# Two transformer blocks on one core: attention A moved off GpSimd, with its steps cut and ordered anew

## The chip, the core and the metric

The kernel runs on one core of a Trainium2 chip. The engines are named as the profile names them: PE (TensorE, matrix products into the eight banks of PSUM, ps0 to ps7), DVE (VectorE), ACT (ScalarE), POOL (GpSimd), and SP (SyncE), which issues all DMAs here. Each engine works through its own list of instructions in order and stops at a wait on a semaphore; nothing behind the waiting instruction can pass it. The metric is the time of one execution in microseconds (us), lower is better.

## What is computed

The first block has a layer with differential attention ("attention A"), a feed-forward part, a layer with banded attention ("attention B"), and another feed-forward part. The second block has a gated mixer and a feed-forward part. The sequence has 512 rows of 1024 features. The change touches attention A:

```python
def diff_attention(x, w_qkv, lam_params, subln_g, w_o, lambda_init):
    qkv = x @ w_qkv                       # 8 heads, each with two q/k halves of 64 and v of 128
    q = apply_rope(q, cos, sin) * (A_HEAD_DIM ** -0.5)      # * 0.125
    k = apply_rope(k, cos, sin)
    for i in range(s // Q_BLOCK):         # 4 blocks of 128 queries, keys 0 .. 128*(i+1)
        sc = jnp.einsum('bqhmd,bkhmd->bhmqk', q[:, q0:kend], k[:, :kend])
        p = jax.nn.softmax(jnp.where(allowed, sc, neg), axis=-1)
        a = p[:, :, 0] - lam * p[:, :, 1]
        outs.append(jnp.einsum('bhqk,bkhe->bqhe', a, v[:, :kend]))
    o = rms_norm(o, subln_g) * (1.0 - lambda_init)
    return o.reshape(b, s, D_MODEL) @ w_o
```

Its output is added to the scaled input, and a layer norm follows.

## The kernel before

Every weight matrix is read in tiles of 128 x 1024 numbers (512 KB). A tile is split in two on the chip: ACT rounds it to `whi` (the step `split`, L989), DVE forms the remainder `wlo` (L1269), and PE multiplies three times (L527 to L529): high by high, and the two mixed products. Activations are split in the same way (`xh`, `xl`, `hh`, `hl`). Six places hold split tiles, and splits are issued four tiles ahead of their use.

A class `Plan` writes one list of steps for all engines. Each engine walks the whole list and emits its own share of each step, so the order of the list is the order of every engine's program. In attention A the list is woven from two strands.

The filler strand is made of pieces. Each piece is six matmuls of 512 columns. The q projection of a head takes four pieces, the k projection four more; after the heads' projections come groups of the output product with `a_w_o` ("rows", one block of 256 inputs for one block of 128 rows per piece). When a projection is done, the step `post` applies the rotation: DVE multiplies the PSUM bank by the sine table in two halves into `tmp` (L1297, L1298) and by the cosine table into q or k (L1301); POOL adds the two (L1616). For q, POOL then makes two copies that are masked by halves (L1621, L1624), since the two softmaxes of a head share one product of full height. Each `post` is followed by a `split` of a later tile.

The attention strand is the table `ORDER_A`, run once for each head; a dash stands for one piece of filler, a small letter for a step of the head before:

- `S0` to `S3`: the scores of query block i. PE makes two products of 128(i+1) columns (L783), DVE blanks a corner (L1451), takes row maxima (L1454) and scales them by -0.125 (L1457), ACT takes the exponentials with their sums (L1132).
- `F0` to `F3`: the shares. DVE inverts the sums (L1465), multiplies one by minus lambda (L1468), scales the first exponential (L1469) and adds the second, scaled (L1472).
- `T0` to `T3` (`t3` for the head before): PE transposes the shares (L793), ACT copies them out of PSUM (L1139).
- `w`: PE multiplies v by the transposed shares (L803), ACT squares the result (L1149).
- `n`: PE sums the squares with a matrix of ones (L813), ACT forms the inverse root (L1155, L1157), DVE scales the head by it (L1478), ACT rounds the head to `hh` (L1159), DVE forms `hl` (L1480).

A bank is taken in rotation; those that gather over several steps (projections, output rows, the result of `w`) are held and skipped. Before PE writes a bank it waits for the operation that read it last; for the bank of `w` that is L1478 (the semaphore `of`). `AHEAD_A` pieces of filler run before the first head's turn. After the last head come the output product's remaining rows and the layer norm.

Of the kernel before, what the change touches and what calls it, by code (L numbers as in the profile page):

```python
# [10 lines left out]
ALU = mybir.AluOpType  # L11
ACT = mybir.ActivationFunctionType
AX = mybir.AxisListType.X
# [15 lines left out]
AHEAD_A = 8  # L29
ORDER_A = "- t3 - S0 S1 F0 w F1 - T0 S2 T1 S3 F2 - - - F3 n T2 -".split()  # L30
# [20 lines left out]
class Plan:  # L51
# [152 lines left out]
    def rows(self, kind, source, row0, nk, k_first=0, hh=True, norm=None, group=0):  # L204
# [3 lines left out]
        for nh in range(2):  # L208
            ends = nh == 1 and norm is not None
            if ends:  # L210
                runs = [blocks]
                self.step("table", SQRT)
            elif nh == 1:
                runs = [[k] for k in blocks[:-n]] + [blocks[-n:]]
            else:
                runs = [[k] for k in blocks]
            out, taken = {}, {}
            for run in runs:
                for t in range(4):
                    if ends and t == 3:  # L220
                        self.waiting = True
                    for k0 in run:
                        first, last = k0 == blocks[0], k0 == blocks[-1]
                        if first and (t == 0 or ends):
                            for u in [t] if ends else range(4):
                                out[u] = Rows(kind, nh, u, self.bank(hold=True), self.count(kind), norm, group)
                        if ends and norm >= 4 and last and t == 3:
                            self.feat(norm, 1)
                            self.xsplit(norm, 1)
                            self.step("ln", norm, 2)  # L230
                        if t == 0:
                            taken[k0] = self.take("rows", *source, row0 + k0, nh)
                        r = out[t]
                        signal = last or t == 3
                        ready = max(self.h[k0], self.h[k0 + 1]) if hh else None
                        self.step("rows", r, k0, taken[k0], first, last, signal, ready)
                        if signal:
                            r.value = self.count("rows") + 1
                        if t == 3:
                            self.done(taken[k0], "rows", r.value)  # L240
                        if ends and first and t == 3 and norm >= 4:
                            self.feat(norm, 0)
                            self.xsplit(norm, 0)
                        elif ends and first and t >= 2 and norm < 4:
                            self.feat(norm, t - 2)
                            self.xsplit(norm, t - 2)
                            if t == 3:
                                self.step("ln", norm, 2)
                        if last:
                            self.held.discard(r.bank)  # L250
                            self.step("rows_post", r)
                            if ends and t < 2:
                                if norm >= 4 and t == 1:
                                    self.step("yscale", norm, 0)
                                self.step("ln", norm, t)
                            elif ends and t == 2 and norm >= 4:
                                self.step("yscale", norm, 1)
                        yield
# [1586 lines left out]
```

## Time and profile before

| What | Value |
|---|---|
| time before, median of 3 runs | 1864.07 us (1862.79 to 1864.3) |
| the profiled execution's own time | 1865.22 us |
| its span, first to last instruction | 1863.5 us |
| mean granted clock of PE | 0.995 |
| PE busy | 1819.0 us, 98% |
| DVE busy | 903.0 us, 48% |
| ACT busy | 654.3 us, 35% |
| POOL busy | 65.9 us, 4% |
| DMA | 176.6 MB, mean 95 GB/s |

The span leaves 1.7 us of the profiled time outside it. PE is busy nearly throughout; the places where it is not are short and lie for the most part in the first 260 us. Busy time says which engine has work, not who waits for whom; for that the waits and the chain are read, stretch by stretch.

### The profile page before, as it was taken

The page shows a single profiled execution, that of the slowest core. Times are in us where ns is not written, and L with a number is a line of the kernel's source. Part 1 is how long each engine was busy: PE and PEld are TensorE (multiplying, and loading weights), DVE is VectorE, ACT ScalarE, POOL GpSimd, SP SyncE. Part 2 cuts the span into 40 slices and gives each one's busy share as a digit, 9 for nine tenths or more (in the row PEclk, how much of TensorE's full clock was granted, in tenths as well). Part 3 has the DMA queues.
Part 4 walks back from the last instruction along what each step waited for, and adds up shares of the span by engine and source line. Part 5 has one row for each costly group of instructions (what it writes and reads, how often), then busy time and mean ns, then how long its engine had stood idle before and what let it go on. Part 6 is the DMA issues. An engine that isn't in the chain of part 4 may idle for free.

```text
span 1863.5 us, 21342 instructions
## 1 busy us (share of the span) xinstructions
PE 1819.0 (98%) x8624; PEld 1464.8 (79%) x8624; DVE 903.0 (48%) x1540; ACT 654.3 (35%) x1080; POOL 65.9 (4%) x68
## 2 busy tenths in 40 slices
PE   8989889999999999999999999999999999999998
PEld 6766669888888896666788888888877798888886
DVE  3588865333333634555743333338343573334343
ACT  4344433312222234554232231233445453323241
POOL 0332200000000000000000000000000000000000
PEclk9999999999999999999999999999999999999999
DMA  8322232333423342222233323353221424242321
GB/s 273 108 74 79 72 90 69 102 91 102 113 79 94 121 125 74 80 68 62 69 102 102 91 93 100 101 148 92 63 68 57 124 92 112 70 113 79 102 90 46
DMA packets 217881, 176.60 MB, mean 95 GB/s; under 512 B 8963, under 2 KB 177829, under 8 KB 217782
## 3 DMA queue, kind: packets, MB, share of 16 engines
q1 hardware_dynamic: 217782, 175.23, 31.3%
q8 instruction: 69, 1.13, 0.3%
q14 instruction: 30, 0.25, 0.0%
HBM read 173.07 MB, written 7.38 MB: 97 GB/s over the span
## 4 chain that ended last, share of the span: by engine, by line
PE 91%; DVE 6%; ACT 2%; issue 1%; DMA 0%; SPq 0%
PE ps L527 27%; PE ps L529 27%; PE ps L528 27%; PE ps L823 2%; PE ps L833 1%; PE ps L783 1%; PE ps L845 1%; DVE wlo L1269 1%; PE ps L722 1%; DVE stat L1454 1%; PE ps L934 0%; DVE arena L1301 0%; DVE arena L1297 0%; DVE arena L1298 0%; PE ps L793 0%
## 5 line engine op out<-in xcount | busy, mean ns | idle before, releaser
L527 PE MATMUL ps<-xh,whi 128*128 128x512 f32 (+1 forms) x1176 | 442.3, 376 | 0.0
L529 PE MATMUL ps<-xh,wlo 128*128 128x512 f32 (+1 forms) x1176 | 431.4, 367 | 0.0
L528 PE MATMUL ps<-xl,whi 128*128 128x512 f32 (+1 forms) x1176 | 431.0, 367 | 0.0
L1269 DVE TENSOR_TENSOR wlo<-raw,whi 128x1024 fp32r<-128x1024 f32 x236 | 285.5, 1228 | 272.6 <-ACT whi L989 272.1
L989 ACT ACTIVATE whi<-raw 128x1024 fp32r<-128x1024 f32 x236 | 244.5, 1051 | 133.3 <-PE ps L529 104.4
L527 PE MATMUL ps<-whi,hh 128*128 128x512 f32 x648 | 256.4, 396 | 5.5 <-DVE hl L1480 3.7
L529 PE MATMUL ps<-whi,hl 128*128 128x512 f32 x648 | 253.0, 390 | 0.0
L527 PEld LDWEIGHTS ps<-xh,whi 128*128 128x128 f32 x1176 | 222.7, 189 | 38.4 <-issue 4.5
L528 PE MATMUL ps<-wlo,hh 128*128 128x512 f32 x648 | 252.9, 390 | 0.0
L529 PEld LDWEIGHTS ps<-xh,wlo 128*128 128x128 f32 x1176 | 221.9, 189 | 36.9
L528 PEld LDWEIGHTS ps<-xl,whi 128*128 128x128 f32 x1176 | 222.2, 189 | 36.4 <-issue 2.9
L527 PEld LDWEIGHTS ps<-whi,hh 128*128 128x128 f32 x648 | 122.4, 189 | 32.1 <-issue 7.7
L529 PEld LDWEIGHTS ps<-whi,hl 128*128 128x128 f32 x648 | 122.0, 188 | 25.8
L528 PEld LDWEIGHTS ps<-wlo,hh 128*128 128x128 f32 x648 | 122.2, 189 | 24.9 <-issue 0.5
L527 PE MATMUL ps<-xh,extra 128*128 128x512 f32 (+1 forms) x328 | 116.2, 354 | 2.0 <-DVE xl L1282 2.0
L529 PE MATMUL ps<-xh,extra 128*128 128x512 f32 (+1 forms) x328 | 115.7, 353 | 0.0
L528 PE MATMUL ps<-xl,extra 128*128 128x512 f32 (+1 forms) x328 | 115.7, 353 | 0.0
L1346 DVE SCALAR_TENSOR_TENSOR x<-x,ps 128x512 f32<-128x512 f32 x64 | 43.9, 685 | 114.9 <-PE ps L529 114.9
L1011 ACT ACTIVATE arena<-ps 128x512 f32<-128x512 f32 x44 | 26.3, 598 | 199.4 <-PE ps L529 199.4
L1014 ACT ACTIVATE hh<-arena 128x512 fp32r<-128x512 f32 x44 | 27.8, 632 | 194.9 <-DVE arena L1307 194.9
L1269 DVE TENSOR_TENSOR extra<-raw,extra 128x1024 fp32r<-128x1024 f32 x53 | 64.5, 1222 | 56.4 <-ACT extra L989 56.4
L527 PE MATMUL ps<-whi,xh 128*128 128x512 f32 x192 | 78.7, 410 | 8.4 <-DVE wlo L1269 8.4
(200 smaller groups left out, 2117.2 us busy)
## 6 DMA issues: line engine op xcount, KB each, us to landing
raw<-in_ffn_w_in SPq DMA_DIRECT2D x88, 512.0 KB, 4.0
raw<-in_w_ff SPq DMA_DIRECT2D x64, 512.0 KB, 4.2
raw<-in_ffn_w_out SPq DMA_DIRECT2D x44, 512.0 KB, 3.8
raw<-in_a_w_qkv SPq DMA_DIRECT2D x24, 512.0 KB, 5.1
raw<-in_w_in SPq DMA_DIRECT2D x20, 512.0 KB, 3.8
raw<-in_kv_w SPq DMA_DIRECT2D x16, 512.0 KB, 4.6
bias_skewed<-bias_rows SPq DMA_DIRECT2D x8, 640.0 KB
raw<-in_a_w_o SPq DMA_DIRECT2D x8, 512.0 KB, 5.2
```

Source lines behind the costliest of these rows:

```text
L527: e.matmul(o, ah, bh, start=start, stop=False)
L528: e.matmul(o, ah, bl, start=False, stop=False)
L529: return e.matmul(o, al, bh, start=False, stop=stop)
L722: m = e.transpose(ps[b][:, k * 128:k * 128 + 128], src[:, c:c + 128], ident[:])
L783: e.matmul(ps[b][:, 0:n], q[:, i * 128:i * 128 + 128], k[:, 0:n], start=True, stop=True).then_inc(s.scores, 1)
L823: e.matmul(ps[b][:, 0:n], q[c, i * 128:i * 128 + 128], k[c, 0:n], start=True, stop=True).then_inc(s.scores_b, 1)
L833: m = e.transpose(ps[b][:, j * 128:j * 128 + 128], e_[:, j * 128:j * 128 + 128], ident[:])
L989: e.activation(self.parts(m)[0], self.raw[:, m % RAW, :], ACT.Copy).then_inc(s.hi, 1)
L1011: e.activation(self.silu_out[n % 2], ps[b][:], ACT.Silu).then_inc(s.silu, 1)
L1014: e.activation(self.hh[:, job.arg[-1], :], self.h_out[n % 2], ACT.Copy).then_inc(s.hh, 1)
L1269: e.tensor_tensor(lo, self.raw[:, m % RAW, :], f32(hi), ALU.subtract).then_inc(s.lo, 1)
L1346: e.scalar_tensor_tensor(x[:, t, c], x[:, t, c], 1.0 if r.group else ALPHA, ps[b][:], ALU.mult, ALU.add).then_inc(s.res, 1)
```

## The change

All of GpSimd's share of attention A moves. DVE adds the two parts of the rotation itself (L1330 of the changed kernel), behind the three multiplications. ACT makes the two masked copies of q (L1018, L1020), and the masks now hold 0.125, so that the scores come out scaled. The row maxima are written negated by the reduction itself, one for each of the two scores, and the multiplication by -0.125 falls away. The shares are cut in two steps: `R` (DVE inverts and multiplies by minus lambda, then ACT scales the first exponential, L1154) and `F` (DVE adds the second). The end of a head is cut in three: `n` (PE's sum and ACT's inverse root), `m` (DVE's scaling, ACT's rounding, and the bank of `w` given back to the rotation) and `l` (`hl`). The table has eight dashes instead of seven, and four pieces run ahead instead of eight.

The output product's order is written as one list; in attention A three pieces of its second half are drawn before the last four of its first half, so that 15 pieces of it, not 12, can fill attention A. The order within the other stages stays, but for the loading of ACT's square-root table (later by three pieces) and the numbers of the banks.

```diff
-AHEAD_A = 8
-ORDER_A = "- t3 - S0 S1 F0 w F1 - T0 S2 T1 S3 F2 - - - F3 n T2 -".split()
+AHEAD_A = 4
+ORDER_A = "- t3 - S0 S1 w R0 R1 - F0 F1 T0 S2 n - T1 - R2 m S3 F2 - - T2 l R3 F3 -".split()
...
         blocks = [(k_first + k) % nk for k in range(0, nk, 2)]
         n = min(3, len(blocks))
-        for nh in range(2):
...
+        left = [(0, t, k) for k in blocks for t in range(4)]
+        if norm is not None:
+            right = [(1, t, k) for t in range(4) for k in blocks]
...
+        order = left[:-4] + right[:3] + left[-4:] + right[3:] if early else left + right
...
-        out = self.rows("res", ("a_w_o", 0), 0, 8, norm=1)
+        out = self.rows("res", ("a_w_o", 0), 0, 8, norm=1, early=True)
...
-            for _ in range(12):
+            for _ in range(15):
...
                 elif name == "n":
-                    self.step("norm_a", g, av[g], self.bank(), self.block(g))
+                    self.step("norm_a", g, self.bank())
+                elif name == "m":
+                    self.step("heads_a", g, av[g], self.block(g))
                     self.held.discard(av[g])
+                elif name == "l":
+                    self.step("low_a", g, self.h[g] - 1)
...
+                elif name[0] == "R":
+                    self.step("ratios_a", g, int(name[1]))
...
-                if job.kind == "gate":
+                if job.kind == "q_a":
+                    h = job.arg
+                    q0, q1, _ = self.qk_a[h % 3]
+                    w.wait_ge(s.rope, 2 * h + 1)
+                    w.wait_ge(s.mask, 16)
+                    e.activation(q1, q0, ACT.Copy, scale=self.masks[:, 1:2]).then_inc(s.half, 1)
+                    w.wait_ge(s.half, h + 1)
+                    e.activation(q0, q0, ACT.Copy, scale=self.masks[:, 0:1]).then_inc(s.halves, 1)
+                elif job.kind == "gate":
...
                 for m, b in enumerate(banks):
-                    w.wait_ge(s.nb, z + 1)
+                    w.wait_ge(s.nb, 2 * z + m + 1)
...
-                                 bias=self.stat[:, c + 2 + m:c + 3 + m], scale=0.125,
+                                 bias=self.stat[:, c + 2 + m:c + 3 + m],
...
+            elif what == "ratios_a":
+                h, i = arg
+                z, e0 = 4 * h + i, self.e_a[(4 * h + i) % 2][0][:, 0:(i + 1) * 128]
+                w.wait_ge(s.ratio, z + 1)
+                e.activation(e0, e0, ACT.Copy, scale=self.stat[:, 8 * z + 6:8 * z + 7]).then_inc(s.share0, 1)
...
                     e.tensor_tensor(dst, ps[b][:], self.cosb, ALU.mult).then_inc(s.cos, 1)
+                    w.wait_ge(s.dve, own)
+                    w.wait_ge(s.cos, u + 1)
+                    e.tensor_tensor(dst, dst, self.tmp, ALU.add).then_inc(s.rope, 1)
...
-                    e.reduce_max(stat[:, c + m:c + m + 1], ps[b][:, 0:n], AX).then_inc(s.dve, 1)
-                    own += 1
-                w.wait_ge(s.dve, own)
-                e.tensor_scalar(stat[:, c + 2:c + 4], stat[:, c:c + 2], -0.125, None, ALU.mult).then_inc(s.nb, 1)
+                    e.tensor_reduce(stat[:, c + 2 + m:c + 3 + m], ps[b][:, 0:n], AX, ALU.max,
+                                    negate=True).then_inc(s.nb, 1)
+
+            elif what == "ratios_a":
+                h, i = arg
+                z = 4 * h + i
+                r = stat[:, z * 8 + 6:z * 8 + 8]
+                w.wait_ge(s.exp, 2 * z + 2)
+                e.reciprocal(r, stat[:, z * 8 + 4:z * 8 + 6]).then_inc(s.ratio, 1)
+                w.wait_ge(s.ratio, z + 1)
+                e.tensor_tensor(r[:, 1:2], r[:, 1:2], self.nlam, ALU.mult).then_inc(s.ratio1, 1)
...
-                e.tensor_scalar(e0, e0, r[:, 0:1], None, ALU.mult).then_inc(s.dve, 1)
-                own += 2
-                w.wait_ge(s.dve, own)
-                e.scalar_tensor_tensor(e0, e1, r[:, 1:2], e0, ALU.mult, ALU.add).then_inc(s.p, 1)
...
+                w.wait_ge(s.share0, z + 1)
+                w.wait_ge(s.ratio1, z + 1)
+                e.scalar_tensor_tensor(e0, e1, stat[:, z * 8 + 7:z * 8 + 8], e0, ALU.mult, ALU.add).then_inc(s.p, 1)
+
+            elif what == "heads_a":
+                h, b, block = arg
                 w.wait_ge(s.rstd, h + 1)
                 w.wait_ge(s.hl, h)
                 e.scalar_tensor_tensor(self.of_a, ps[b][:], self.g8, self.sq_a, ALU.mult, ALU.mult).then_inc(s.of, 1)
+
+            elif what == "low_a":
+                h, block = arg
...
-            elif what == "post" and arg[0].kind in ("q_a", "k_a"):
...
-                e.tensor_tensor(dst, dst, self.tmp, ALU.add).then_inc(s.rope, 1)
...
-                    e.tensor_scalar(q1, q0, self.masks[:, 1:2], None, ALU.mult).then_inc(s.pool, 1)
...
-                    e.tensor_scalar(q0, q0, self.masks[:, 0:1], None, ALU.mult).then_inc(s.halves, 1)
```

The first place is ACT's program between two heads in the middle of attention A. Before, from the split behind `S3` to the exponentials of the next `S0` and `S1` (L1132 exponential, L989 `whi` of a tile, L1155 to L1159 the end of a head, L1139 copy of transposed shares):

```order
L989 ACTIVATE whi<-raw 128x1024 [waits s_job,s_raw0]
L1155 ACTIVATE arena<-ps5,small 128x512 [waits s_ss]
L1157 ACTIVATE arena<-arena 128x512 [waits s_ss_ln]
L1159 ACTIVATE hh<-arena 128x512 [waits s_of]
L1139 ACTIVATE arena<-ps6 128x3x128 [waits s_turn]
L1139 ACTIVATE arena<-ps7 128x4x128 [waits s_turn]
L989 ACTIVATE whi<-raw 128x1024 [waits s_job,s_raw1]
L1132 ACTIVATE arena,stat<-ps1,stat 128x128 [waits s_nb]
L1132 ACTIVATE arena,stat<-ps2,stat 128x128
L1132 ACTIVATE arena,stat<-ps3,stat 128x256 [waits s_nb]
L1132 ACTIVATE arena,stat<-ps4,stat 128x256
```

Of the change (L1159 and L1146 are now the copy and the exponential, L1154 the scaling of a share, L1018 and L1020 the masked copies, L995 `whi`):

```order
L1159 ACTIVATE arena<-ps1 128x3x128 [waits s_turn]
L1154 ACTIVATE arena<-arena,stat 128x512 [waits s_ratio]
L1018 ACTIVATE arena<-arena,small 128x512 [waits s_rope]
L1020 ACTIVATE arena<-arena,small 128x512 [waits s_half]
L995 ACTIVATE whi<-raw 128x1024 [waits s_job,s_raw1]
L1159 ACTIVATE arena<-ps3 128x4x128 [waits s_turn]
L1146 ACTIVATE arena,stat<-ps4,stat 128x128 [waits s_nb]
L1146 ACTIVATE arena,stat<-ps5,stat 128x128 [waits s_nb]
L1146 ACTIVATE arena,stat<-ps6,stat 128x256 [waits s_nb]
L1146 ACTIVATE arena,stat<-ps7,stat 128x256 [waits s_nb]
L1169 ACTIVATE arena<-ps0 128x512 [waits s_av]
L1154 ACTIVATE arena<-arena,stat 128x128 [waits s_ratio]
```

The two masked copies, which wait for the rotation of q, now stand ahead of `whi`, and `whi` ahead of the copy for the last transpose, on which `w` waits. The scaling for `F3` stands behind the copy for `T2`.

The second place is PE's program in one head, from `w` to the scores of `S3`. Before (L803 `w`, L793 transposes, L783 scores, L527 the first matmul of a piece's group):

```order
L803 MATMUL ps6<-arena 128x512 [waits s_cos,s_at]
...
L793 MATMUL ps0<-ident,arena 128x128 [waits s_p]
L783 MATMUL ps1<-arena 128x384
L783 MATMUL ps2<-arena 128x384 [waits s_exp]
L793 MATMUL ps3<-ident,arena 128x128 [waits s_exp,s_p]
...
L783 MATMUL ps4<-arena 128x512 [waits s_exp]
L783 MATMUL ps5<-arena 128x512 [waits s_exp]
L527 MATMUL ps7<-xh,whi 128x512
```

Of the change (L809 `w`, L799 transposes, L789 scores, L819 the sum of squares, L532 the filler):

```order
L809 MATMUL ps2<-arena 128x512 [waits s_exp,s_at]
...
L799 MATMUL ps3<-ident,arena 128x128 [waits s_p]
L789 MATMUL ps5<-arena 128x384
L789 MATMUL ps6<-arena 128x384 [waits s_exp]
L819 MATMUL ps7<-arena,ones 128x512 [waits s_exp,s_square]
L532 MATMUL ps4<-xh,whi 128x512
...
L799 MATMUL ps0<-ident,arena 128x128 [waits s_exp,s_p]
...
L532 MATMUL ps1<-xh,whi 128x512 [waits s_exp,s_lo]
...
L789 MATMUL ps2<-arena 128x512 [waits s_of]
L789 MATMUL ps3<-arena 128x512 [waits s_at]
L532 MATMUL ps1<-xh,whi 128x512
```

Before, no score of this head writes the bank of `w`, ps6. Of the change, `S3` takes ps2, the bank that `w` wrote for the head before, and waits for `of`; four pieces stand between `w` and it, and PE has nothing else it may do while it waits.

## Rows read from the trace of the kernel before

**Rows 1.** The page, part 1: busy us (share of the span) and instructions.

```profile
PE 1819.0 (98%) x8624; PEld 1464.8 (79%) x8624; DVE 903.0 (48%) x1540; ACT 654.3 (35%) x1080; POOL 65.9 (4%) x68
```

**Rows 2.** By stretch: length, busy time (instructions), clock, DMA share, GB/s.

```profile
54.70:257.00 202.30, 179.93 (x746) 128.71 (x744) 157.86 (x374) 88.09 (x215) 54.10 (x32) 0.98 0.25 78
257.00:1863.50 1606.50, 1592.71 (x7688) 1298.04 (x7688) 727.08 (x1146) 545.74 (x843) 10.79 (x28) 1.00 0.31 91
```

**Rows 3.** Waits of PE in attention A: us in total, times, longest.

```profile
PE ps L793 <- DVE arena L1472: 5.9, 7, 1.3
PE ps L813 <- DVE arena L1301: 5.1, 3, 2.3
PE ps L527 <- DVE hl L1480: 3.7, 1, 3.7
```

**Rows 4.** Timeline of DVE, two posts: start, us, [idle <-releaser].

```profile
71.18 0.69 DVE L1297 TENSOR_TENSOR arena<-ps,arena 64x512 f32<-64x512 f32 x1 [2.21 <-PE ps L529]
...
76.62 0.69 DVE L1297 TENSOR_TENSOR arena<-ps,arena 64x512 f32<-64x512 f32 x1 [2.21 <-PE ps L529]
```

**Rows 5.** The chain of waits in order of time: start us, us, what.

```profile
190.39 1.72 PE ps L783 x4
...
198.25 1.07 DVE stat L1468
...
247.45 2.21 PE ps L803 x8
...
253.32 0.70 ACT arena L1155
254.04 0.64 ACT arena L1157
254.70 0.76 DVE arena L1478
255.48 0.64 ACT hh L1159
256.15 0.70 DVE hl L1480
```

**Rows 6.** DVE groups while POOL rests: count | busy, mean ns | idle.

```profile
L1269 DVE TENSOR_TENSOR wlo<-raw,whi 128x1024 fp32r<-128x1024 f32 x3 | 3.7, 1226 | 2.5 <-ACT whi L989 2.5
...
L1472 DVE SCALAR_TENSOR_TENSOR arena<-arena,stat 128x512 f32<-128x512 f32 x2 | 1.5, 751 | 0.1
L1454 DVE TENSOR_REDUCE stat<-ps 128x1 f32<-128x512 f32 x2 | 1.4, 691 | 0.1
...
L1468 DVE TENSOR_TENSOR stat<-stat,small 128x1 f32<-128x1 f32 x4 | 0.6, 159 | 0.1
...
L1454 DVE TENSOR_REDUCE stat<-ps 128x1 f32<-128x128 f32 x2 | 0.6, 292 | 0.1
```

**Rows 7.** Groups of ACT in the same stretch.

```profile
L989 ACT ACTIVATE whi<-raw 128x1024 fp32r<-128x1024 f32 x4 | 4.2, 1049 | 0.0
...
L1149 ACT ACTIVATE arena<-ps 128x512 f32<-128x512 f32 x2 | 1.2, 598 | 3.1 <-PE ps L803 3.1
...
L1139 ACT ACTIVATE arena<-ps 128x384 f32<-128x384 f32 x2 | 0.9, 474 | 0.0
L1132 ACT ACTIVATE arena<-ps,stat 128x256 f32<-128x256 f32 x2 | 0.9, 470 | 0.5 <-DVE stat L1457 0.5
```

**Rows 8.** DVE groups from 70 to 275 us, all shapes together.

```profile
L1469 DVE TENSOR_SCALAR arena<-arena,stat 128x128 f32<-128x128 f32 (+3 forms) x32 | 15.6, 488 | 0.0
...
L1468 DVE TENSOR_TENSOR stat<-stat,small 128x1 f32<-128x1 f32 x32 | 8.7, 272 | 1.2
L1457 DVE TENSOR_SCALAR stat<-stat 128x2 f32<-128x2 f32 x32 | 7.2, 226 | 1.1
```

**Rows 9.** Busy time by stretch, just after two long waits of PE.

```profile
219.00:222.50 3.50, 3.41 (x8) 2.17 (x9) 2.36 (x4) 1.30 (x2) 1.26 (x1) 0.54 0.02 5
...
256.40:260.00 3.60, 3.02 (x8) 2.42 (x9) 1.74 (x3) 3.57 (x4) 0.00 (x0) 0.53 0.09 22
```

More of the change, by code:

```diff
@@ L200, in projections, with rows @@
             self.run(self.quarters(*w))
-    def rows(self, kind, source, row0, nk, k_first=0, hh=True, norm=None, group=0):
+    def rows(self, kind, source, row0, nk, k_first=0, hh=True, norm=None, group=0, early=False):
         blocks = [(k_first + k) % nk for k in range(0, nk, 2)]
         n = min(3, len(blocks))
-        for nh in range(2):
+        left = [(0, t, k) for k in blocks for t in range(4)]
+        if norm is not None:
+            right = [(1, t, k) for t in range(4) for k in blocks]
+        else:
+            right = [(1, t, k) for k in blocks[:-n] for t in range(4)] + [
+                (1, t, k) for t in range(4) for k in blocks[-n:]]
+        order = left[:-4] + right[:3] + left[-4:] + right[3:] if early else left + right
+        out, taken = {}, {}
+        for nh, t, k0 in order:
+            first, last = k0 == blocks[0], k0 == blocks[-1]
@@ L209, in rows @@
             ends = nh == 1 and norm is not None
-            if ends:
-                runs = [blocks]
+            if first:
+                out[nh, t] = Rows(kind, nh, t, self.bank(hold=True), self.count(kind), norm, group)
+            if ends and last and t == 0:
                 self.step("table", SQRT)
[L213 to L258, printed above, removed]
@@ new lines, in rows @@
+            if ends and first and t == 3:
+                self.waiting = True
+            if ends and norm >= 4 and last and t == 3:
+                self.feat(norm, 1)
+                self.xsplit(norm, 1)
+                self.step("ln", norm, 2)
+            if t == 0:
+                taken[nh, k0] = self.take("rows", *source, row0 + k0, nh)
+            r, tile = out[nh, t], taken[nh, k0]
+            signal = last or t == 3
+            ready = max(self.h[k0], self.h[k0 + 1]) if hh else None
@@ new lines, in rows @@
+            self.step("rows", r, k0, tile, first, last, signal, ready)
+            if signal:
+                r.value = self.count("rows") + 1
+            if t == 3:
+                self.done(tile, "rows", r.value)
+            if ends and first and t == 3 and norm >= 4:
+                self.feat(norm, 0)
+                self.xsplit(norm, 0)
+            elif ends and first and t >= 2 and norm < 4:
+                self.feat(norm, t - 2)
+                self.xsplit(norm, t - 2)
+                if t == 3:
+                    self.step("ln", norm, 2)
@@ L260, in half_rows @@
+            if last:
+                self.held.discard(r.bank)
+                self.step("rows_post", r)
+                if ends and t < 2:
+                    if norm >= 4 and t == 1:
+                        self.step("yscale", norm, 0)
+                    self.step("ln", norm, t)
+                elif ends and t == 2 and norm >= 4:
+                    self.step("yscale", norm, 1)
+            yield
     def half_rows(self, kind, col):
@@ L1151, in scalar @@
             elif what == "norm_a":
-                h, _, b, block = arg
+                h, b = arg
                 w.wait_ge(s.eps, 2)
@@ L1296, in vector @@
                         w.wait_ge(s.rope, u)
[L1297 to L1298 removed]
+                    e.tensor_tensor(self.tmp[0:64, :], ps[b][64:128, :], self.sinb[64:128, :],
+                                    ALU.mult).then_inc(s.dve, 1)
+                    e.tensor_tensor(self.tmp[64:128, :], ps[b][0:64, :], self.sinb[0:64, :],
+                                    ALU.mult).then_inc(s.dve, 1)
+                    own += 2
                     if h >= 3:
@@ L1607, in gpsimd @@
                 before = (s.ext, 1)
-            elif what == "post" and arg[0].kind in ("q_a", "k_a"):
-                job = arg[0]
-                h, which = job.arg, int(job.kind == "k_a")
-                q0, q1, k = self.qk_a[h % 3]
-                dst, u = k if which else q0, 2 * h + which
-                w.wait_ge(*before)
-                w.wait_ge(s.cos, u + 1)
-                e.tensor_tensor(dst, dst, self.tmp, ALU.add).then_inc(s.rope, 1)
-                before = (s.rope, u + 1)
-                if not which:
-                    w.wait_ge(s.mask, 16)
-                    w.wait_ge(s.rope, u + 1)
-                    e.tensor_scalar(q1, q0, self.masks[:, 1:2], None, ALU.mult).then_inc(s.pool, 1)
-                    own += 1
-                    w.wait_ge(s.pool, own)
-                    e.tensor_scalar(q0, q0, self.masks[:, 0:1], None, ALU.mult).then_inc(s.halves, 1)
-                    before = (s.halves, h + 1)
             elif what == "bias":
```

21 lines of the change are left out of this document (7 added, 14 removed).

## The prediction

> **What bounds the kernel now.** I read busy time first: PE 1819 of 1863.5 us, 98% [rows 1]. The change cannot shorten PE's work, since every product stays, so all that can move is PE's waiting. The busy time by stretch says where that is: from 257 us on PE is idle 13.8 us in 1606; in attention A, 54.7 to 257 us, it is idle 22.4 in 202.3, while DVE works 157.9 us there, 78% [rows 2]. The waits name DVE: 5.9 us for the share (L1472) before the transposes, 5.1 us in 3 waits where PE needs the bank that the rotation (L1301) had yet to read, and 3.7 us once at the end, for `hl` of the last head [rows 3]. So attention A is a loop in which PE and a crowded DVE wait for one another, and everything behind it only shifts.
>
> **What the change takes from DVE.** Out go the scaling of the first exponential, 15.6 us in 32, and of the maxima, 7.2 us [rows 8]. In come 16 sums of 512 columns; L1480, with two inputs in SBUF of that size, took 0.70 [rows 5], so 11.2. Net 11.6 us. POOL costs DVE something too: L1468 took 1.07 us once, beside 0.16 while POOL rests, and 0.27 in the mean [rows 5, 6, 8]; its 32 alone hold 3.6 us of that, and I put all such stretching of the remaining instructions at 4 to 7 us. DVE's work falls from 158 to about 140 us. POOL's path (about 50 us of work) is gone.
>
> The Trainium skill ("SBUF — State Buffer", Who interferes with whom) has DVE and GpSimd share a port pair as an exclusive lock; the row of 1.07 agrees. "Perfetto Trace Analysis" (Optimizing Scalar/DVE Operations) advises moving work from a saturated DVE to ScalarE. By that rule alone PE's waits for DVE would shrink, the first rival below.
>
> **What it adds, and where it waits.** ACT gets 16 masked copies and 32 scalings, about 25 us on 88 [rows 2]. ACT has room in the sum, but not in order. I follow one full head (1 to 6), from its `T0` to the next one's. A result reaches the next engine 0.03 to 0.06 us after its record's end; behind a matmul I add 0.2. A piece is 1.36 us: two posts start 5.44 us apart with four pieces between [rows 4].
>
> 1. PE: `T0` 0.1, `S2` 1.3 (three quarters of the 1.72 of `S3`), `n` 0.86, the fourth piece of k 1.36, 0.2 to land: 3.8 [rows 4, 5].
> 2. DVE: rotation of k, four times 0.69, 2.75; `wlo` 1.22; two small ones 0.36; `m` 0.76: 5.1 [rows 4 to 6]. In DVE's order `m` stands behind the post and the split.
> 3. PE: `S3` takes the bank of `w` and waits for `m`. PE reached it four pieces after `w`, at 16.4 us of the head, and `m` ends at 20.2: PE idles 3.8 us. Then `S3` 1.7, about 0.4 until matmuls run at pace behind it, two pieces 2.7, `T2` and landing 0.5: 5.4.
> 4. ACT copies `T2` 0.47 and only then scales for `F3`, 0.64 (as L1157); DVE adds, 0.75; gaps 0.1: 2.0 [rows 5 to 7].
> 5. DVE rotates q: 2.75.
> 6. ACT makes the two masked copies, which wait for the finished rotation: 1.3 with a gap. Only then comes `whi` 1.05; DVE, standing at `wlo`, waits 2.4 us, then 1.22: 3.7 [rows 6, 7]. Behind `whi` stands also the copy of `t3`, so `w` on PE starts 2.1 us late. Before, POOL masked beside all this and `whi` waited for nothing.
> 7. DVE blanks and reduces `S0` and `S1`: 2 x 0.29, 2 x 0.43 (between 0.29 and 0.69), 4 x 0.16: 2.1 [rows 6].
> 8. ACT: last exponential with its sum 0.7 [0.47 in rows 7], the square 0.6, the scaling 0.3; DVE's add 0.35; gaps: 2.0. `T0` comes 1.2 us late.
>
> Sum 26.8 us a head. PE's own work in it: 8 pieces 10.9, scores 4.3 (1.72 x 10/4), `w` 2.2, transposes 1.1, `n` 0.86: 19.3 [rows 4, 5]. So 7.5 us of waiting a head.
>
> The scaling on ACT shows nowhere before for SBUF operands; the bounds are 0.28 to 0.48 (the PSUM copy of up to 384 columns, 0.47, [rows 7]) and 0.64 for 512 columns, and I take 0.3 for 128 columns and 0.64 for 512. The masked copies lie between 0.60 (L1149) and 0.64 (L1157); I take 0.64. Either end moves a head by 0.2 us.
>
> **The sum.** Twelve pieces ahead of head 0 (8 of its own, 4 of `AHEAD_A`): 16.3. Head 0, with no `t3`, `w`, `n`: PE work 15.8, and 6.1 of waiting, since its first maxima stand behind rotation, masks, `whi` and `wlo` of q of head 1: 21.9. Six heads: 161. Head 7 and the end: 11 pieces 15.0, attention 8.4, `T3`, `w` and `n` of the head before 3.5, `S3` waiting for `m` 3.4, the end's chain ACT 0.70, 0.64, DVE 0.76, ACT 0.64, DVE 0.70 and 0.8 around it, 4.2 [rows 5]: 34.6. The end's chain is hidden no better than before: all 15 pieces are used up before `n`. Together 233.8 us, up to the first row block that needs the last head, where before took 202.3 [rows 2]. Three pieces more are done by then, 4.1 us. Net +27.4. The layer norm's first rows follow its sums closer than before (one piece instead of four between): 0 to +1.5, taken as 0.
>
> PE's clock: after two of PE's long waits (2.3 and 3.7 us) the stretches of 3.5 us show it at 0.54 and 0.53, close to 1.2 GHz instead of 2.4 [rows 9], and each costs up to 1.7 us of work. The stage before holds two such falls; mine has eight waits of 3 us or more. Bounds 0 and 13.6; I take two again, 3.4, because some long waits of before left the clock alone. The Trainium skill ("TensorE: Matmul & The Clock Gate", HAM oscillation — how this bites in real kernels) warns of repeated idle gaps; by it the sum would take the upper bound, 1905.
>
> The profiled execution took 1865.22, 1.15 over the median. 1865.22 + 27.4 + 3.4 - 1.15 = 1894.9, so 1895.
>
> **The rivals.**
> A. Faster, by the port and the lighter DVE. DVE's 140 us fit well under PE's work, and PE's waits for DVE (the 5.9 and 5.1 of [rows 3] and some 5 more) go, with a fall of the clock: 1864 - 16 - 2 = 1846. It needs the masked copies and `m` to end before they are asked for. Against it: DVE would be idle when PE asks, and steps 3 and 6 are waits of order, not of load. Chance 0.13.
> B. Slower, but only by one of the two order waits. If `S3` finds its bank free (a post ending earlier), 2.6 us a head go (the wait, less what steps 3 and 4 would then meet at DVE) over seven heads: 1895 - 18 = 1877. Chance 0.25.
> C. The two cancel: 3 us a head lost, as many won by the port. 1864, chance 0.05.
> D. The clock falls in nearly every head, 13.6 instead of 3.4: 1905. Counted with the forecast, together 0.57.
>
> The change does what it says in any of these; that it wouldn't has no chance of its own.
>
> The range: 1867 to 1908 leaves out most of A and C below and a little above. A measurement of this kernel tells 0.2%, 3.7 us, from no change. Faster by more 0.13, within 0.05, slower 0.82.
>
> **What would show it.** PE waiting for DVE's `m` (L1507) before L789 of 512 columns, over 3 us, in heads 1 to 7: step 3. ACT idle before L1018, DVE idle 2.4 us before L1292 with ACT's L995 as releaser, once a head: step 6. PE waiting for ACT's L1159 at L809. Rows L1330 at 0.69. The squares' products (L819) 26 to 28 us apart. L1493 at 0.16 throughout: the port. DVE busy near 140 us in the stage. If L789 never waits for L1507, step 3 is wrong; if `wlo` follows the rotation at once, step 6 is; if heads stand 20 us apart, A holds.

## The result

| | before | after |
|---|---|---|
| time, median | 1863.94 us | 1907.02 us (1906.5 to 1908.51, 4 runs) |
| ratio to before | | 1.0234, 95% interval 1.0216 to 1.0251 |
| profiled execution, its span | 1865.22, 1863.5 us | 1908.51, 1906.8 us |
| mean granted clock of PE | 0.995 | 0.983 |
| attention A, from 54.7 us to the first product that needs the last head | 202.3 us | 249.6 us |
| PE idle in it | 22.4 us | 47.3 us |
| half-clock stretches in it | 3, 10.2 us | 12, 51.2 us |

The half-clock stretch at the end of the stage is counted whole, though most of it lies behind the end. The change is slower by 43.1 us, 12 us more than the 1895 forecast and inside the range. Part 1 of the page after, as [rows 1]:

```profile
PE 1837.3 (96%) x8624; PEld 1473.4 (77%) x8624; DVE 887.6 (47%) x1492; ACT 684.8 (36%) x1128; POOL 11.8 (1%) x36
```

PE's busy time rose by 18.3 us with the same 8624 products; POOL's fell from 65.9 to 11.8. Where, the stretches tell, as in [rows 2]:

```profile
54.70:304.30 249.60, 202.25 (x764) 140.43 (x762) 144.77 (x328) 120.68 (x266) 0.00 (x0) 0.90 0.22 68
304.30:1906.80 1602.50, 1588.76 (x7670) 1294.87 (x7670) 724.72 (x1144) 543.66 (x841) 10.77 (x28) 1.00 0.31 91
```

Behind attention A the program takes 1602.5 us, before 1606.5: it has three pieces less to do (4.1 us at 1.36). So all of the loss lies in the stage: 249.6 - 202.3 - 4.1 = 43.2. Of this, idle time of PE is 47.3 - 22.4 = 24.9, and longer busy time 202.2 - 179.9 - 4.1 = 18.2. The second part goes with the clock, 0.90 in the mean, before 0.98. The waits of PE, from 50 to 310 us, as [rows 3]:

```profile
PE ps L789 <- DVE arena L1507: 22.5, 7, 3.5
PE ps L809 <- ACT arena L1159: 11.9, 6, 2.0
PE ps L799 <- DVE arena L1501: 6.9, 4, 4.6
PE ps L532 <- DVE hl L1512: 3.7, 1, 3.7
PE ps L799 <- DVE arena L1327: 2.3, 1, 2.3
```

`S3` waits for `m` in seven heads (3.5 us in six, 1.6 in the last), `w` for the copy of `t3` in six. What DVE itself waits for:

```profile
DVE wlo L1292 <- ACT whi L995: 26.8, 14, 3.2
DVE ps L1480 <- PE ps L789: 26.3, 24, 2.2
DVE arena L1501 <- ACT arena L1154: 24.2, 15, 3.0
```

The first of these in the kernel before, from 50 to 310 us too:

```profile
DVE wlo L1269 <- ACT whi L989: 9.5, 12, 3.3
```

DVE, which was crowded before, now stands and waits: for `whi` 26.8 us instead of 9.5, for PE's scores 26.3, for ACT's scaling 24.2. Two stretches of the stage, the wait of one `S3` and what follows it (columns as in [rows 2]; compare [rows 9]):

```profile
143.00:146.80 3.80, 0.34 (x2) 0.00 (x0) 3.60 (x7) 1.13 (x2) 0.00 (x0) 1.00 0.00 0
146.80:150.30 3.50, 3.48 (x5) 1.51 (x5) 0.80 (x2) 1.07 (x2) 0.00 (x0) 0.51 0.59 147
```

PE did 0.34 us of work in 3.8, at full clock, and then ran 3.5 us at half clock (1.2 of 2.4 GHz). The chain of waits through most of this head:

```profile
144.70 1.13 DVE wlo L1292
...
146.02 0.76 DVE arena L1507
...
146.82 3.65 PE ps L789 x4
...
153.61 0.49 ACT arena L1159
154.10 0.62 ACT arena L1154
...
155.53 0.69 DVE arena L1320
...
157.77 0.70 DVE arena L1330
...
158.50 0.73 ACT arena L1018
...
159.27 0.60 issue
159.88 1.05 ACT whi L995
...
160.95 1.23 DVE wlo L1292
```

The head's time is a single file of steps from engine to engine: `wlo`, `m` (L1507), `S3` (L789), the copy of `T2` (L1159) and the scaling behind it (L1154), the rotation of q (L1320 to L1330), the masked copies (L1018; L1020 lies in the 0.60 shown as issue), `whi`, `wlo`. And the rows that answer to the bounds, with count, busy time and mean ns:

```profile
L1330 DVE TENSOR_TENSOR arena<-arena 128x512 f32<-128x512 f32 x12 | 8.3, 692 | 1.3
...
L1493 DVE TENSOR_TENSOR stat<-stat,small 128x1 f32<-128x1 f32 x29 | 4.6, 159 | 1.0
```

```profile
L1154 ACT ACTIVATE arena<-arena,stat 128x512 f32<-128x512 f32 x8 | 5.7, 714 | 0.0
...
L1018 ACT ACTIVATE arena<-arena,small 128x512 f32<-128x512 f32 x6 | 4.3, 722 | 22.7 <-DVE arena L1330 22.7
L1020 ACT ACTIVATE arena<-arena,small 128x512 f32<-128x512 f32 x6 | 4.3, 721 | 0.2
...
L1154 ACT ACTIVATE arena<-arena,stat 128x128 f32<-128x128 f32 x7 | 2.8, 396 | 0.0
```

### The profile page after: what moved, and what is told of

Its sections match the earlier page's. It is cut to its first block, busy times and chain, and to the rows that moved or that the text cites. A ratio compares the mean times of both kernels' runs of the same rounds, so it can differ in the third digit from the quotient of the medians.

```text
span 1906.8 us, 21339 instructions
## 1 busy us (share of the span) xinstructions
PE 1837.3 (96%) x8624; PEld 1473.4 (77%) x8624; DVE 887.6 (47%) x1492; ACT 684.8 (36%) x1128; POOL 11.8 (1%) x36
## 4 chain that ended last, share of the span: by engine, by line
PE 91%; DVE 5%; ACT 2%; issue 1%; DMA 0%; SPq 0%; DVEq 0%
PE ps L532 27%; PE ps L534 27%; PE ps L533 27%; PE ps L829 2%; PE ps L789 2%; PE ps L839 1%; PE ps L851 1%; PE ps L728 1%; PE ps L809 1%; DVE wlo L1292 1%; ACT whi L995 1%; DVE arena L1327 1%; DVE arena L1320 1%; DVE arena L1322 1%; DVE arena L1330 0%
## 5 line engine op out<-in xcount | busy, mean ns | idle before, releaser
L532 PE MATMUL ps<-xh,whi 128*128 128x512 f32 (+1 forms) x1176 | 449.1, 382 | 0.0
L995 ACT ACTIVATE whi<-raw 128x1024 fp32r<-128x1024 f32 x236 | 244.3, 1050 | 121.8 <-PE ps L534 89.7
L532 PE MATMUL ps<-whi,hh 128*128 128x512 f32 x648 | 257.3, 397 | 5.5 <-DVE hl L1512 3.7
L532 PEld LDWEIGHTS ps<-xh,whi 128*128 128x128 f32 x1176 | 224.5, 191 | 41.3 <-issue 7.4
L532 PEld LDWEIGHTS ps<-whi,hh 128*128 128x128 f32 x648 | 122.4, 189 | 32.8 <-issue 8.5
L532 PE MATMUL ps<-xh,extra 128*128 128x512 f32 (+1 forms) x328 | 116.2, 354 | 2.0 <-DVE xl L1305 2.0
L532 PE MATMUL ps<-whi,xh 128*128 128x512 f32 x192 | 78.9, 411 | 8.5 <-DVE wlo L1292 8.5
```

The lines of the kernel that those rows point to most:

```text
L532: e.matmul(o, ah, bh, start=start, stop=False)
L995: e.activation(self.parts(m)[0], self.raw[:, m % RAW, :], ACT.Copy).then_inc(s.hi, 1)
```

## The experiments

The theory: two waits of order make the loss, `S3` for the bank of `w` and `whi` behind the masked copies, and the clock adds to them. A rival: the work moved to ACT and DVE costs time wherever it stands. Another: the new order itself costs time. Line numbers differ from kernel to kernel; the letters of the steps are the same. "Late masks" is this step: ACT's masked copies leave `post` and stand as their own step `M` ahead of `R2`. For each run the table shows the stage as above, from 54.7 us to the first product that needs the last head. "Slower pace" is busy time over 176.2 us, which the tenth experiment's profile needed with no half-clock stretch, less 4.1 where three more pieces lie in the stage. The figure is good to about 1 us: experiment 11 comes out at -0.8. Each profile is of one execution, which can lie up to 4 us from the median in its row (that of 10 took 1858.0 us, that of 8 1865.5). A half-clock stretch that begins within 1.5 us of the end of the stage is counted whole.

| kernel | median us | ratio, 95% interval | PE idle | slower pace | half-clock stretches us |
|---|---|---|---|---|---|
| before | 1863.94 | | 22.4 | 3.7 | 10.2 |
| the change | 1907.02 | 1.0216 to 1.0251 | 47.3 | 21.9 | 51.2 |
| 1 bank | 1882.37 | 1.0081 to 1.0112 | 32.9 | 8.5 | 20.5 |
| 2 late masks | 1884.68 | 1.0095 to 1.0126 | 35.6 | 10.8 | 27.3 |
| 3 both | 1863.81 | 0.9989 to 1.0008 | 20.5 | 4.3 | 13.7 |
| 4 old order | 1884.34 | 1.0093 to 1.0123 | 34.2 | 10.1 | 23.9 |
| 5 is 3, scaling on DVE | 1861.23 | 0.9973 to 0.9991 | 20.5 | 2.1 | 17.1 |
| 6 is 3, early scores of head 0 | 1856.70 | 0.9948 to 0.9973 | 17.7 | 0.8 | 6.8 |
| 7 is 4, scaling on DVE | 1875.91 | 1.0049 to 1.0076 | 28.0 | 5.1 | 17.1 |
| 8 before, negated maxima | 1863.03 | 0.9979 to 0.9997 | 18.1 | 5.2 | 17.1 |
| 9 is 1, masks on POOL | 1860.45 | 0.9967 to 0.9986 | 17.9 | 0.9 | 6.8 |
| 10 is 7, late masks | 1861.73 | 0.9982 to 1.0000 | 20.4 | 0 | 0 |
| 11 is 3, 5 and 6 | 1858.02 | 0.9954 to 0.9979 | 18.0 | -0.8 | 6.8 |
| 12 is 11, two pieces behind `w` | 1875.75 | 1.0046 to 1.0072 | 32.6 | 2.7 | 10.2 |

**1. The bank of `w` kept from `S3`.** The bank goes back to the rotation only once `S3` has taken its two:

```diff
-                    self.held.discard(av[g])
+                    if h == 8:
+                        self.held.discard(av[g])
...
                     self.step("scores_a", g, int(name[1]), [self.bank(), self.bank()])
+                    if name == "S3" and h:
+                        self.held.discard(av[h - 1])
```

> The changed kernel (1907 us) with one edit: the bank of w is given back to the rotation only after S3 has taken its two banks, so S3 of a head no longer waits for the scaling of the head before (of). Nothing is left out of the computation. Theory O (the loss is waits of order in in-order programs): the 3.5 us wait before S3 goes in seven heads, and with it the fall of PE's clock that follows each one; per head about 2.4 us of chain and 1.7 us of slow clock, so 1907 - 29 = 1878 us, with the clock falling at most twice in the stage. Rival L (the work that was moved to DVE and ACT is itself too much for them, the order only shows it): PE waits the same time elsewhere, 1900 us or more. Rival C (the clock falls come from the other waits too): the waits before S3 go but the falls stay, about 1890 us.

Measured: 24.6 us less than the change. The waits of the stage:

```profile
PE ps L802 <- DVE arena L1504: 14.9, 11, 4.6
PE ps L812 <- ACT arena L1162: 11.8, 6, 2.0
```

No wait for `of` is left. L802 (transposes) now waits 14.9 us for the share, the next in line; `w`'s wait for ACT stays at 11.8. So step 3 of the prediction is shown. Idle time fell by 14.4 us and the slower pace by 13.4. The time is 4 us above the 1878 of the theory: five half-clock stretches are left instead of two, two of them at waits of 2.0 us before `w`, as the third expectation had it in part.

**2. Late masks.**

```diff
-ORDER_A = "- t3 - S0 S1 w R0 R1 - F0 F1 T0 S2 n - T1 - R2 m S3 F2 - - T2 l R3 F3 -".split()
+ORDER_A = "- t3 - S0 S1 w R0 R1 - F0 F1 T0 S2 n - T1 - M R2 m S3 F2 - - T2 l R3 F3 -".split()
...
+            elif what == "masks_a":
```

> The changed kernel with one edit: ACT makes the two masked copies of q half a head later, between the rounding of a weight tile behind T1 and the scaling for R2, where ACT sat idle 2.4 us, and no longer ahead of whi and of the copy for t3. The bank of w stays as in the change. Theory O: DVE's 2.5 us wait for whi behind the rotation of q goes in seven heads, and PE's 2.0 us wait before w with it; the wait before S3 stays at 3.5 us with its clock falls: 1907 - 17 = 1890 us. Rival L: DVE and ACT are simply full, 1903 us or more. A third way: the 2.4 us won only lengthen the wait before S3, since PE comes there earlier, in which case 1900 us.

Measured: 22.3 us less, 5 more than expected. PE's wait at `w` is gone, DVE's for `whi` fell from 26.8 to this, level with the 9.5 of the kernel before, while `S3`'s stays:

```profile
DVE wlo L1303 <- ACT whi L1005: 9.4, 7, 3.2
```

```profile
PE ps L799 <- DVE arena L1518: 22.4, 7, 3.5
```

Of the six waits of 3.5 us only three stand beside a half-clock stretch here, in the change all six did.

**3. Both edits together.**

> Both edits together: the bank of w kept from S3, and the masked copies half a head later. Theory O: the two gains add, as they lie one behind the other on the loop through a head: 1907 - 29 - 17 = 1861 us, a little below the kernel before (1864), heads about 22 us apart. Rival L: at least 1885 us, DVE near 90% busy in the stage. Between them: 1870 us if a third wait of order (the scaling for F3 behind the copy for T2) takes over.

Measured: 43.2 us less, the whole loss and no more; the ratio to before holds 1. Alone the two edits give 24.6 and 22.3, 46.9 in sum. PE's waits in the stage:

```profile
PE ps L812 <- DVE arena L1515: 14.3, 13, 4.6
PE ps L545 <- DVE hl L1526: 3.7, 1, 3.7
PE ps L812 <- DVE arena L1341: 2.3, 1, 2.3
```

The transposes waiting for the share, 1.2 us a head and 4.6 once in head 0, and the end. Heads are 21.6 us apart. The rival that the moved work itself costs time wherever it stands falls: the work is all there, and nothing of the loss is left. Whether the new order gains something that the work takes back, this run does not separate.

**4. The moved work in the old order.** The change's ACT and DVE work, with the table close to that of before:

```diff
-AHEAD_A = 4
-ORDER_A = "- t3 - S0 S1 w R0 R1 - F0 F1 T0 S2 n - T1 - R2 m S3 F2 - - T2 l R3 F3 -".split()
+AHEAD_A = 8
+ORDER_A = "- t3 - S0 S1 R0 F0 w R1 F1 - T0 S2 T1 S3 R2 F2 - - - R3 F3 n m l T2 -".split()
```

and 12 pieces of the output product instead of 15, in the order of before.

> The work as the change divides it among the engines (no POOL, negated maxima, scaling on ACT), but in the order of the kernel before: R directly ahead of F, the end of a head undivided, eight pieces ahead, seven a head, and the output rows not begun early. Theory O: no S3 wait for the head's scaling; the masked copies stand ahead of whi in most heads (up to 2.4 us each, about 12 us), DVE is lighter by some 17 us and free of POOL's port (10 us back): 1866 us, between 1858 and 1874. Rival L: the moved work alone costs 25 us or more, 1890 us.

Missed by 18 us: 1884.34. The old order has no conflict over the bank of `w`, yet takes 20 us more than before. DVE's waits:

```profile
DVE arena L1501 <- ACT arena L1154: 23.9, 32, 1.9
DVE wlo L1292 <- ACT whi L995: 19.8, 15, 3.0
```

`F` follows `R` at once there, so each of the 32 scalings on ACT is waited for, 0.75 us in the mean, and `whi` behind the masked copies costs DVE 19.8 us as well. I had priced both too low. With the same work the old order is 22.7 us faster than the order of the change, but 20.5 slower than experiment 3.

**5. The scaling back on DVE, on top of 3.**

```diff
+                e0 = self.e_a[z % 2][0][:, 0:(i + 1) * 128]
...
+                e.tensor_scalar(e0, e0, r[:, 0:1], None, ALU.mult).then_inc(s.share0, 1)
```

in `R` on DVE, and none on ACT.

> Both earlier edits (bank kept from S3, masked copies half a head later; 1863.8 us) and the first exponential scaled on DVE again, in the step R, instead of on ACT. DVE gets 1.5 us a head more (0.28 to 0.48 each by the rows of the kernel before) and no longer waits 12.3 us in all for ACT's scaling. If the round trip through ACT is what still sets the pace: heads 21 instead of 21.6 us apart, 1859 us. If DVE's load sets it: 1868 us or more. In between, no difference that can be measured: 1862 to 1866 us.

Measured: 2.6 us less than 3, the intervals just overlapping; heads 21.3 us apart instead of 21.6. The round trip to ACT costs 0.3 us a head where other steps lie between `R` and `F`. The 32 scalings' records sum to 12.2 us, but DVE's busy time rose by only 8.1 (144.26 to 152.31): records on DVE overlap by about a tenth of a microsecond each.

**6. The scores `S0` and `S1` of head 0 a piece earlier, on top of 3.** They are issued ahead of the last piece of `AHEAD_A`, and with it of the post of the q projection of head 1:

```diff
-        for _ in range(AHEAD_A):
+        for n in range(AHEAD_A):
+            if n == AHEAD_A - 1:
+                self.mask()
+                for i in range(2):
+                    self.step("scores_a", 0, i, [self.bank(), self.bank()])
```

> Both earlier edits (1863.8 us) and S0 and S1 of head 0 put one piece earlier, ahead of the post of q of head 1, so that DVE takes their maxima before that rotation and the split behind it. If head 0's waits (4.6 and 2.3 us before two transposes) come from that order: the 4.6 us wait goes, the falls of PE's clock around it (10 us at half in the first head) for the most part too: 1855 us, faster than the kernel before. If DVE is merely overloaded there, the wait moves to the next transposes: 1862 us or more.

Measured: 7.1 us less than 3. The longest wait of the transposes falls from 4.6 to 3.5 us, idle time by 2.8, and of the two stretches near 80 us (10.2 us at half clock) one of 3.4 is left.

**7. The scaling on DVE in the old order, on top of 4**, by the edit of 5.

> The old order with the moved work (1884.3 us), but the scaling of the first exponential on DVE again. In that run DVE waited 32 times for ACT's scaling, 23.9 us in all, with F directly behind R. Theory R (in the old order the loss is the round trip through ACT): 23.9 us of waiting against 12.2 us of DVE's own work, so 1872 us, and down to 1866 where falls of the clock go with it. Theory M (the loss is the masked copies ahead of whi, 19.8 us of DVE waiting for whi): 1880 us or more. Theory L (DVE's load): 1885 us or more, as DVE gets work back.

Measured: 8.4 us less than 4, three times what the same edit gave in the new order, and between the 1872 of the first theory and the 1880 of the second: the round trip is a part of the loss. DVE still waits 19.7 us for `whi`.

**8. Only the negated maxima, in the kernel before.**

```diff
-                    e.reduce_max(stat[:, c + m:c + m + 1], ps[b][:, 0:n], AX).then_inc(s.dve, 1)
...
-                e.tensor_scalar(stat[:, c + 2:c + 4], stat[:, c:c + 2], -0.125, None, ALU.mult).then_inc(s.nb, 1)
+                    e.tensor_reduce(stat[:, c + 2 + m:c + 3 + m], ps[b][:, 0:n], AX, ALU.max,
+                                    negate=True).then_inc(s.nb, 1)
```

with 0.125 in the masks.

> The kernel before with one part of the change alone: maxima written negated by the reduction, one wait for each of the two scores, no multiplication by -0.125, and 0.125 in POOL's masks. DVE loses 7.2 us of work on its path to the exponentials. If DVE's path sets attention A's pace before the change, as the waits say: 1864 - 5 = 1859 us. If PE's waits have other ends: 1862 to 1865 us.

Missed: 0.9 us less than before, not 5. PE's idle time did fall, by 4.3, but its profile has 17.1 us at half clock in the stage instead of 10.2, and 3.4 more behind it, near 1403 us. That is the profile of an execution of 1865.5 us. Five of the eleven executions took 1859.1 to 1859.8, the 1859 that was expected, at a mean granted clock of 0.995; the other six, at 0.992 to 0.994, took 1863.0 to 1865.5. The kernel before took 1862.6 us or more in every execution, at 0.995 and 0.996, so the lighter path gains where the clock does not fall below that.

**9. The masked copies on POOL, right behind the rotation, on top of 1.** The sum of the rotation stays on DVE:

```diff
+            elif what == "post" and arg[0].kind == "q_a":
...
+                e.tensor_scalar(q1, q0, self.masks[:, 1:2], None, ALU.mult).then_inc(s.half, 1)
+                w.wait_ge(s.half, h + 1)
+                e.tensor_scalar(q0, q0, self.masks[:, 0:1], None, ALU.mult).then_inc(s.halves, 1)
```

> The changed kernel with S3's banks kept clear of w (the first experiment, 1882.4 us), and the two masked copies of each piece made by GpSimd right behind the rotation instead of by ScalarE ahead of whi; the sum of the rotation stays on VectorE. If the masked copies cost only by standing ahead of whi on ScalarE, it comes out with the version that makes them on ScalarE in a late step (1863.8 us): 1860 to 1868 us, VectorE's wait for whi down from about 27 us of the stage to about 9. If GpSimd's copies hold VectorE up by their use of the memory of the core at the same time, VectorE's busy time between 80 and 240 us rises above the 118 us of the late version, and the time is 1870 us or more.

Measured: 1860.45, as by the theory of order. It is 3.4 us less than 3; in its profile the longest wait of the transposes, in head 0, is 2.0 us instead of 4.6. From 70 to 275 us:

```profile
L1642 POOL TENSOR_SCALAR arena<-arena,small 128x512 f32<-128x512 f32 x7 | 16.8, 2397 | 113.3 <-DVE arena L1325 113.3
L1644 POOL TENSOR_SCALAR arena<-arena,small 128x512 f32<-128x512 f32 x7 | 11.0, 1564 | 0.7
```

```profile
L1488 DVE TENSOR_TENSOR stat<-stat,small 128x1 f32<-128x1 f32 x32 | 5.1, 160 | 1.1
```

POOL's first copy, which runs beside `wlo`, takes 2.40 us where the kernel before took 1.63 in the mean; DVE pays nothing for it: its product of one column stays at 0.16, `wlo` at 1.22, and its busy time from 80 to 240 us is 119.5, with late masks on ACT 118.3.

**10. Late masks in the old order, on top of 7**, with `M` after `F2`.

> The old order of the moved work, the scaling of the first exponential on VectorE (1875.9 us without the next edit), and the masked copies taken from ahead of whi and put on ScalarE as a late step of their own. If the copies ahead of whi are what is left of the loss under the old order (VectorE waited 19.7 us there for whi), it is 1858 to 1865 us, the wait of wlo for whi gone, and the half-clock stretches back to about three. If something else in the old order holds it up, it stays at 1872 us or more.

Measured: 14.2 us less than 7, level with before. The stage, and PE's largest waits in it:

```profile
54.70:251.21 196.51, 176.15 (x746) 127.03 (x744) 152.52 (x358) 101.92 (x232) 0.00 (x0) 1.00 0.26 81
```

```profile
PE ps L809 <- DVE arena L1513: 5.3, 3, 3.1
PE ps L829 <- DVE arena L1337: 5.0, 3, 2.3
```

The clock reads 1.00, and no half-clock stretch is in the stage, though PE waited 3.1 us once and 3.7 at the end. The profile is of the fastest of ten executions, 1858.0 us at a mean clock of 0.997; the others took 1860.5 to 1866.0 at 0.993 to 0.996. So the masked copies were the rest of the loss in the old order. The new order carries all of the moved work at the time of before once they stand late, the old one with the scaling on DVE.

**11. The edits of 5 and 6 together, on top of 3.**

> The version with S3's banks clear of w and late masked copies (1863.8 us), with both of the gains found on top of it: the first exponential scaled on VectorE (2.6 us alone) and the scores of head 0 one piece earlier (7.1 us alone). If the two are independent: 1854 us, 1851 to 1857. If the earlier head 0 gained through the clock stretches that the scaling shifts again: 1856 to 1862 us.

Measured: 1858.02, just outside the first expectation and within the second. The scaling on DVE adds nothing on top of 6, though heads are 21.3 us apart again; its profile has 10.2 us of half clock behind the stage, near 1315 and 1370 us, where that of 6 has 3.4.

**12. Two pieces between `w` and `T0`, on top of 11**, taken from between `n` and `T1`:

```diff
+ORDER_A = "- t3 - S0 S1 w R0 R1 - F0 F1 - T0 S2 n T1 - M R2 m S3 F2 - - T2 l R3 F3 -".split()
```

> The combined version (1854 us expected) with two pieces of projection instead of one between w and the transposes T0 of the next head, one fewer elsewhere. The waits of the transposes for the last softmax step (14 us over the stage in the version with late masked copies, up to 4.6 us each) would be covered: heads 20.3 us apart instead of 21.3, 1846 us. If the waits only move to the place from which the piece is taken: no better than the combined version, 1853 us or more.

Missed: 1875.75, 17.7 us more than 11, heads 24 us apart. PE's waits:

```profile
PE ps L818 <- DVE arena L1522: 16.1, 9, 2.5
PE ps L808 <- DVE arena L1346: 12.7, 6, 2.1
```

```profile
DVE wlo L1311 <- ACT whi L1014: 29.7, 11, 3.4
```

The transposes (L818) wait as long as in 11 (14.4), and the scores of `S2` (L808) now wait 2.1 us in six heads for the rotation (L1346): they take the bank that the projection of k has just filled. It is the fault of `S3` again, with another bank. Why the transposes gained nothing, the trace of 11 tells: the expectation had the wrong ones. In it PE waits 1.5 us a head before `T2`, the three transposes behind `S3`, and not at all before `T0`, where the second piece was put. Here the wait before `T2` is 1.8 to 1.9 us. The late exponentials of `S2` also hold up ACT's `whi` behind them, and DVE waits for it 29.7 us, in 11 12.2.

## Why the prediction was right

The forecast case held, and both waits of order are shown by edits that take them away one at a time. Rival A is excluded: the squares' products (L819) stood 25 to 30 us apart, but for the last. B fell too, since both waits were there; it priced the bank's wait at 18 us, and experiment 1 measured 24.6, its clock included. C fell. What came nearest was D, counted with the forecast.

Step by step, in the head from 137.9 us (`T0`) to 166.0:

| steps | forecast us | measured us |
|---|---|---|
| 1, 2: to the end of `m` | 8.9 | 8.9 |
| 3: `S3`, two pieces, `T2` | 5.4 | 6.8 |
| 4: copy, scaling, add | 2.0 | 1.9 |
| 5: rotation of q | 2.75 | 3.0 |
| 6: masked copies, `whi`, `wlo` | 3.7 | 3.7 |
| 7, 8: to the next `T0` | 4.1 | 3.8 |
| sum | 26.8 | 28.1 |

- The waits: `S3` 3.5 (forecast 3.8), `w` 2.0 (2.1), `T0` 0.8 (1.2); 6.3 a head instead of 7.5. Only step 3 is much longer, for its `S3` ran at half clock. The prediction, and the section on the change, have four pieces between `w` and `S3`; there are three, and the wait of 3.8 us that it gives is what its own steps give with three. Over the stage PE idles 24.9 us more than before; the sum had 27.4.
- The term that was mis-sized is the clock: "I take two again, 3.4". It measured 18.2, over the upper bound of 13.6 too. The bound allowed one fall for each of eight waits of 3 us or more. The 3.4 was also added to a time that already holds the three stretches of before, of which the prediction saw two. In the trace of the change there are twelve stretches: two in head 0, one at each of the six `S3` waits of 3.5 us, one at the end, and three more at `w`, after waits of only 2.0; three of the twelve were 6.8 us long, twice the others. Because some waits of before left the clock alone, I took the low end; but before had only three waits over 2.2 us, and all three stood beside a fall [rows 9 show two].
- By the rule on repeated idle gaps of the Trainium skill that the prediction weighed ("TensorE: Matmul & The Clock Gate", HAM oscillation — how this bites in real kernels), the sum was 1905. The measured 1907 agrees with it in the total, in part by luck: the idle time came out 2.5 us lower than in that sum and the clock 4.6 higher. Not every long gap was followed by a fall: of the six waits of 3.5 us in experiment 2 three were, of the waits of 3.1 and 3.7 us in experiment 10 neither. What decides it stays open.
- L1330 at 0.69 us and L1493 at 0.16 came as forecast: the stretching of DVE's instructions beside POOL is gone (128-column scalings took 0.45 us in the mean before and 0.28 in experiment 5). The 1.07 us of L1468, which the prediction read once, stands four times in the trace, as 1.05 to 1.07. No gain in time is seen from it, as DVE now waits for the others. DVE's work fell to 144.8, not 140: the scalings' records overlap, as experiment 5 shows.
- The masked copies took 0.72 us each instead of 0.64, the scaling of 128 columns 0.40 instead of 0.3: about 0.3 us a head.

So the cause of the loss of 43 us is shown: the bank of `w`, 24.6 us taken away alone, and the masked copies ahead of `whi`, 22.3 alone, 43.2 both together. In each of the two about half is idle time and half the slower pace that comes with it. Experiment 6 has the lowest median, 0.4% under before: the change's work and order, without its two waits, and with head 0's scores begun a piece earlier. How much of that the eighth dash, the 15 pieces or the cut steps bring was not taken apart.

## What to carry to other kernels

When work moves to an engine with room, look at what stands behind it in that engine's order: here two copies of 0.7 us held up `whi`, and with it DVE and PE, by 2 to 2.5 us a head, and the same copies a few steps later cost nothing. A rotation of buffers is a set of waits; after each change of an order, follow the bank of each long-lived result to who takes it next. And count the clock beside PE's waits: here 24.9 us more of waiting came with 18.2 of slower pace, and experiments 1 and 2 took away 14.4 with 13.4 and 11.7 with 11.1. It is no rule for a single wait, and the clock can differ between executions of one kernel, so look at more than one.

## What the runs showed of the hardware

- PE's wait of 3.5 us at `S3` was followed by a half-clock stretch in 6 of 6 heads of the change and in 3 of 6 in experiment 2. PE's wait of 2.0 us at `w` was followed by a half-clock stretch in 3 of 6 heads of the change, where the same heads also had a wait of 3.5 us, and in 2 of 6 in experiment 1. A wait of 1.2 us, as in experiment 3, was followed by none in six heads, and in experiment 10 waits of 3.1 and 3.7 us by none either. A stretch began within the wait (at 174.1 us, where PE idled until 175.0) or with its end (146.8).
- The same program's times can lie 4 us apart. Of ten runs of experiment 9 three took 1856.5 to 1857.0 us and seven 1860.4 to 1860.9; of eleven of experiment 8 five took 1859.1 to 1859.8 and six 1863.0 to 1865.5. The mean granted clock goes with it: 0.996 in the three and 0.994 in the seven, 0.995 in the five and 0.992 to 0.994 in the six. An estimate from these: 0.002 less in the mean over 1860 us is 7.4 us more at half clock, which costs 3.7 us of work, so the clock can be the whole difference. The profiled execution of experiment 9 was one of the three; steps of 2 to 4 us between these versions are read with that in mind.
- Where an instruction of DVE and one of POOL worked in SBUF at the same time and one of them was late, it was the one that began second. In the kernel before, POOL's sum (L1616) took 1.26 to 1.27 us where it began first or alone, and 2.02 to 2.14 in the eight cases from 70 us on where it began 0.2 to 0.3 us behind `wlo`; `wlo` took 1.22 us in these, and 2.30 where it began 0.05 us behind POOL's sum. DVE's product of one column took 1.05 to 1.07 us in four cases where it began 1.1 us into POOL's sum, 0.16 otherwise. In experiment 9 POOL's first copy began 0.25 us behind `wlo` and took 2.40 us, the next one 1.56, and DVE lost nothing.
